# Projection tiles moved to the head of the last stage, gate halves on both sides of the last barrier, and a first gather that reads its indices in place

## The reference

```python
g_logits = hf @ w_rg + b_rg; g_sel = argmax(g_logits)       # one of 4 groups
e_logits = (hf @ w_re + b_re)[group g_sel]                  # 8 experts of it
e_val, e_idx = top_k(e_logits, 2)
gate = softmax(e_val) * softmax(g_logits)[g_sel]
# tokens sorted by expert into blocks; for each block of an expert e:
hid = silu(xe @ w_gate[e]) * (xe @ w_up[e]);  yb = hid @ w_down[e]
x = x + (the two experts' rows of each token, times gate)
gate = sigmoid(rmsnorm(x, g_ple) @ w_ple_gate + b_ple_gate)  # 1024 x 1024
x = x + gate * (p @ w_ple_proj)                              # 256 x 1024
y = rmsnorm(x, g_final)
```

## Time and profile before

| what | value |
|---|---|
| median of three runs | 1224.12 us (1223.11 to 1226.31) |
| the profiled execution | 1224.08 us |
| its span in the trace | 1222.0 us |
| TensorE busy | 1091.6 us (89%) |
| VectorE busy | 528.0 us (43%) |
| ScalarE busy | 489.6 us (40%) |
| GpSimd busy | 240.4 us (20%) |
| moved by DMA | 303.45 MB, mean 248 GB/s |

### The profile page before, as it was taken

How to read it: one execution, slowest core, us unless ns; L and a number is a source line. 1 busy time by engine, 2 the same in 40 slices (tenths; PEclk the granted TensorE clock), 3 DMA queues, 4 the chain that set the end, 5 groups by cost and what they waited for, 6 DMA issues and landing times. The chain is left out here.

```text
span 1222.0 us, 17853 instructions
## 1 busy us (share of the span) xinstructions
PE 1091.6 (89%) x5269; PEld 628.7 (51%) x5270; DVE 528.0 (43%) x687; ACT 489.6 (40%) x667; POOL 240.4 (20%) x280
## 2 busy tenths in 40 slices
PE   3799995689769988899999999999999999949997
PEld 2699995567658764333333333333333333317885
DVE  4458895666832217121321321321221221346886
ACT  4433444433421214343542552552552553523333
POOL 1023564243510011011111111111110110112220
PEclk9899997888969988899999999999999999978999
DMA  6031923201202274699899999999999999984651
GB/s 216 25 106 52 256 68 138 75 35 69 87 18 75 104 283 165 254 395 392 313 395 398 363 397 398 360 397 398 364 397 398 360 397 398 396 346 161 237 190 57
DMA packets 150176, 303.45 MB, mean 248 GB/s; under 512 B 12144, under 2 KB 42896, under 8 KB 150139
## 3 DMA queue, kind: packets, MB, share of 16 engines
q1 hardware_dynamic: 135787, 267.83, 59.8%
q0 software_dynamic: 6512, 22.29, 5.2%
q10 hardware_dynamic: 7840, 12.85, 2.8%
HBM read 262.77 MB, written 40.16 MB: 248 GB/s over the span
## 5 line engine op out<-in xcount | busy, mean ns | idle before, releaser
L1742 PE MATMUL ps_gate_up<-weights,x_turned 128*64 128x512 f32 x1568 | 349.5, 598 | 1.4 <-issue 0.7
L105 ACT COPY weights<-raw_weights 128x2048 f32 (+1 forms) x96 | 180.2, 1899 | 104.3 <-issue 47.4
L105 DVE COPY weights<-raw_weights 128x2048 f32 (+1 forms) x96 | 117.9, 1231 | 228.3 <-PE ps_gate_up L1742 96.4
L1742 PEld LDWEIGHTS ps_gate_up<-weights,x_turned 128*64 128x64 f32 x1568 | 109.5, 137 | 206.9 <-issue 205.8
L1755 PE MATMUL ps_y<-weights,h_turned 128*64 128x512 f32 x784 | 180.7, 603 | 2.4 <-ACT h_turned L1658 2.4
L754 DVE SCALAR_TENSOR_TENSOR taps_bank<-a_ext,par,taps_bank 128x640 f32<-128x640 f32 (+1 forms) x152 | 119.7, 787 | 4.0
L1694 DVE TENSOR_TENSOR hidden<-ps_gate_up,act_gate 128x256 f32<-128x256 f32 x49 | 20.8, 424 | 223.0 <-ACT act_gate L1651 223.0
L395 POOL TENSOR_TENSOR conv_pool_taps<-conv_pool_taps,tap_product 128x640 f32<-128x640 f32 (+1 forms) x64 | 91.7, 1433 | 63.4 <-ACT tap_product L485 57.4
L110 POOL COPY token_ids<-item_tokens 128x1 int32 (+1 forms) x49 | 8.9, 183 | 482.9 <-PE ps_x L1729 457.2
L1755 PEld LDWEIGHTS ps_y<-weights,h_turned 128*64 128x64 f32 x784 | 52.6, 137 | 96.0 <-issue 93.4
L485 ACT ACTIVATE tap_product<-a_ext,par 128x640 f32<-128x640 f32 (+1 forms) x80 | 58.1, 744 | 41.5 <-POOL conv_pool_taps L395 27.5
(11 more groups left out here) (273 smaller groups left out, 1567.2 us busy)
## 6 DMA issues: line engine op xcount, KB each, us to landing
raw_weights<-w_exp_gate SPq DMA_DIRECT2D x128, 512.0 KB, 12.3
raw_weights<-w_exp_up SPq DMA_DIRECT2D x128, 512.0 KB, 12.0
raw_weights<-w_exp_down SPq DMA_DIRECT2D x64, 1024.0 KB, 13.0
y_rows<-y_tile ACTq DMA_DIRECT2D x98, 128.0 KB, 5.4
y_rows<-zero_rows SPq DMA_DIRECT2D x16, 512.0 KB, 6.2
x_rows<-x_tile SPq DMA_DIRECT2D x9, 512.0 KB, 2.6
h_rows<-h_tile SPq DMA_DIRECT2D x9, 512.0 KB, 3.0
proj_rows<-projected SPq DMA_DIRECT2D x9, 512.0 KB, 2.7
```

The lines of the kernel that those rows point to most:

```text
L105: copy(S.work[s][:, :], raw).then_inc(S.w_ready[s], 1)
L1742: last = pe.matmul(ps_gu[side[j], :, :], x_t[:, c, side[of]], w[:, :, share(D_EXP, j)], start=(k == 0), stop=(k == KD - 1))
```

## The change

There is a new constant `LATE = 5`. Tiles 0 to 4 are still projected in `routing`. Tiles 5 to 8 are only transposed there, into a buffer `p_late` that outlives the stage. SyncE then loads the projection's weights a second time, as the first transfer of the expert stage, and `late_project` and `late_leave` multiply and copy out one tile each: tile 5 at the end of the expert stage, tiles 6 to 8 at the head of the last stage. These four are never stored to HBM.

In `routing`, all six pieces of the first expert are now copied by ScalarE, VectorE's chain waits for one GpSimd table instead of all of them, and SyncE's loads of the second expert wait for the last transpose instead of the last projection. In `experts` the last stores of `y` are issued after the copy of `h_turned`, and the engines change places for the gate halves: VectorE makes both halves of pieces 0 and 1 before the barrier, ScalarE the high halves of 2 and 3 before it, and VectorE their low halves after it. The first gather reads its indices from the list without the copy.

```diff
+LATE = 5
 def gather_tokens(pool, S, i):
-    pool.tensor_copy(S.ids[:, :], S.item_tokens[:, bass.ds(i, 1)]).then_inc(S.ids_ready, 1)
-    pool.wait_ge(S.ids_ready, i + 1)
-    pool.sem_inc(S.waits_met, 1)
+    if type(i) is int and i == 0:
+        ids = S.item_tokens[:, 0:1]
+    else:
+        ids = S.ids[:, :]
+        pool.tensor_copy(ids, S.item_tokens[:, bass.ds(i, 1)]).then_inc(S.ids_ready, 1)
+        pool.wait_ge(S.ids_ready, i)
+        pool.sem_inc(S.waits_met, 1)
...
+def gate_lo(dve, S, s):
+    dve.tensor_tensor(S.ple_lo[s][:, :], S.raw[:, 0, s, :], S.ple_hi[s][:, :].bitcast(F32), ALU.subtract).then_inc(S.ple_split, 1)
+
+def late_project(pe, S, t, ps):
+    pe.wait_ge(S.proj_w_loaded, 32)
+    for h in range(2):
+        for k in range(PLE // P):
+            half = slice(h * 512, (h + 1) * 512)
+            last = pe.matmul(ps[:, half], S.p_late[:, t - LATE, k, :], S.late_w[:, k, half], start=(k == 0), stop=(k == PLE // P - 1))
+    last.then_inc(S.late_projected, 1)
+
+def late_leave(act, S, t, ps):
+    act.wait_ge(S.late_projected, t - LATE + 1)
+    act.activation(S.late_rows[t - LATE], ps, ACT.Copy).then_inc(S.late_left, 1)
...
@@ routing, SyncE @@
-                for t in range(T - 1):
+                for t in range(LATE):
                     store(t)
-                sp.wait_ge(projected, 2 * T)
+                sp.wait_ge(projected, 2 * LATE)
+                sp.wait_ge(p_turned, T)
                 for s in (0, 1, 2):
                     load_piece(sp, S, s, 1, 1, slice(1, 2))
-                store(T - 1)
...
@@ routing, TensorE @@
                 for t in range(2, 4):
                     turn_p(t + 1)
                     project(t)
+                turn_p(5)
                 pe.wait_ge(to_place, 1)
                 list_tokens(0)
...
                 pe.matmul(flat_tot[:, 0:ITEMS + 1], owners[:, :], S.ident[:, 0:ITEMS + 1], start=True, stop=True).then_inc(placed, 1)
-                for t in range(5, T):
-                    if t + 1 < T:
-                        turn_p(t + 1)
-                    project(t)
+                for t in range(6, T):
+                    turn_p(t)
...
@@ routing, VectorE @@
-                dve.wait_ge(made, 5)
-                ts(past[:, :], limit[:, 0:SIDES - 1], own_lane[:, :], None, ALU.is_le)
-                red(own_side[:, :], past[:, :], ALU.add)
+                dve.wait_ge(made, 1)
                 dve.wait_ge(S.routed, T)
...
-                for s in (GU[1], GU[3], DOWN[1]):
-                    copy_piece(dve, S, 0, s, None)
...
@@ experts: SyncE first, then the end of ScalarE, VectorE and TensorE @@
+                sp.dma_start(S.late_w[:, :, :], ple_proj).then_inc(S.proj_w_loaded, 16)
...
                 iteration(end, final=True)
-                gate_hi(0)
-                gate_hi(1)
+                gate_hi(2)
+                gate_hi(3)
                 leave_y(end)
+                store_y(end)
+                late_leave(act, S, LATE, ps_late)
...
-                for n, s in enumerate((2, 3)):
+                for n, s in enumerate((0, 1)):
...
-                    gate_lo(s)
-                for s in (0, 1):
-                    dve.wait_ge(S.ple_hi_ready, s + 1)
                     dve.wait_ge(w_ready[DOWN[s]], EXPERTS)
-                    gate_lo(s)
+                    gate_lo(dve, S, s)
...
                 down(end, EXPERTS - 1)
+                late_project(pe, S, LATE, ps_late)
...
@@ embedding_gate, ScalarE @@
+                late_leave(act, S, LATE + 1, ps_g[1][:, :])
+                late_leave(act, S, LATE + 2, ps_h1)
                 to_hi(0)
+                late_leave(act, S, LATE + 3, ps_g[1][:, :])
                 square3(0)
...
@@ embedding_gate, VectorE @@
+                gate_lo(dve, S, 2)
+                gate_lo(dve, S, 3)
+                dve.wait_ge(S.ple_split, 6)
                 combine(0, 0)
...
@@ embedding_gate, TensorE @@
+                late_project(pe, S, LATE + 1, ps_g[1])
+                late_project(pe, S, LATE + 2, ps_h1)
                 turn_h(0, 0)
                 turn_h(0, 1)
+                pe.wait_ge(S.late_left, 2)
+                late_project(pe, S, LATE + 3, ps_g[1])
```

More of the change, by code:

```diff
@@ L95, in load_piece, with copy_piece @@
            .then_inc(S.raw_loaded[s], 16)
-def copy_piece(eng, S, n, s, items):
+def copy_piece(eng, S, n, s, items, on_act=None):
     eng.wait_ge(S.raw_loaded[s], n * LANDED[s] + LANDED[s])
@@ L1472, in _ @@
                 dve.sem_inc(to_exp, 1)
+                ts(past[:, :], limit[:, 0:SIDES - 1], own_lane[:, :], None, ALU.is_le)
+                red(own_side[:, :], past[:, :], ALU.add)
                 dve.wait_ge(ranked, 1)
@@ L1600, in _ @@
                 for j in range(SLOTS):
-                    sp.wait_ge(S.proj_stored[j], 16 * len(range(j, TILES, SLOTS)))
+                    sp.wait_ge(S.proj_stored[j], 16 * len(range(j, LATE, SLOTS)))
                 for t in range(2):
@@ L1656, in iteration @@
                         leave_y(i - 1)
+                        if not final:
+                            store_y(i - 1)
                     act.wait_ge(hid_turned, i + 1)
                     act.activation(h_t[:, :, :], ps_h[:, :, :], ACT.Copy).then_inc(ht_ready, 1)
+                    if final:
+                        store_y(i - 1)
                 def gate_hi(s):
@@ L1704, in _ @@
                 for j in range(SLOTS):
-                    dve.wait_ge(S.proj_stored[j], 16 * len(range(j, TILES, SLOTS)))
-                def gate_lo(s):
-                    dve.tensor_tensor(S.ple_lo[s][:, :], S.raw[:, 0, s, :], S.ple_hi[s][:, :].bitcast(F32), ALU.subtract)\
-                       .then_inc(S.ple_split, 1)
-                for n, s in enumerate((2, 3)):
+                    dve.wait_ge(S.proj_stored[j], 16 * len(range(j, LATE, SLOTS)))
+                for n, s in enumerate((0, 1)):
                     dve.wait_ge(S.raw_loaded[s], LANDED[s] * EXPERTS + 16)
@@ L2132, in build @@
             routing(nc, S)
+        S.late_w = sb("late_ple_proj", [P, PLE // P, D])
+        S.late_rows = [w[:, h * D:(h + 1) * D] for w in S.work[3:5] for h in range(2)]
         S.ple_lo += [sb(f"ple_lo{s}", [P, PIECE], F32R) for s in range(2, 4)]
```

85 lines of the change are left out of this document (54 added, 31 removed).

## The result

Compared on one chip, the changed kernel takes 1215.69 us (median of 5, 1212.61 to 1218.64) and the kernel before 1224.12 (5 runs, 1223.09 to 1226.31). The ratio is 0.9928, with a 95% interval from 0.9905 to 0.9951: faster by 0.7%. The profiled execution took 1214.85 us with a span of 1213.1, against 1224.08 and 1222.0 before. The forecast was 1212.7, with a range from 1209.0 to 1216.0.

A forecast was written before the change was run, and what follows sets the result against it. TensorE was taken to pace the expert loop, with loads running ahead. Routing -15.0, loop 0, loop's end 0 and last stage's head +3.6 sum to -11.4 us: 1224.08 becomes 1212.7, range 1209.0 to 1216.0.

The forecast's parts named there:

- rival 2: Last stage: late gathers make TensorE wait and its clock fall again, +2.0 and up to +1.6 more, 1214.7 to 1216.3; chance 0.15.
- Routing: Routing stage: fewer projections let the second expert's loads and the loop start 15.0 us sooner, bounds 14.2 to 15.7.
- the walk from the earlier trace: Routing: ScalarE's queue added up from 471.6 us to when the last transpose can go, 487.9, or 489.4 with a wait.
- the long case: Routing: tile 2's projection again takes 5.32 us instead of 3.5, so ScalarE waits some 1.5 us: last transpose at 489.4.
- VectorE's earlier chain: Routing: waiting for one table, the chain begins about 3.9 us earlier; about 1.9 us of it arrives at TensorE.
- The loop: Expert loop: TensorE paces it and the 1 MB weight reload is absorbed, 0 us, upper bound 2.7.
- Rival 4: Expert loop: the DMA, not TensorE, sets its end, so an earlier start is worth nothing, 1230.4 us; chance 0.04.
- The end of the loop: Barrier before the last stage: TensorE and VectorE end sooner, but the DMA lands the same bytes; 0, -0.4 to +0.5.
- The held gathers: Head of last stage: VectorE's two subtractions hold GpSimd's first two gathers, rows come 2.1 us later, bounds 0 to 3.7.
- rival 1: Head of last stage: the gathers are not held, leaving only +1.5 us there, 1210.6 us; chance 0.22.
- Tile 8 uncovered and the warm clock: Head of last stage: tile 8 ahead of the first gate product costs +3.5 us; TensorE already warm gives back 2.0.

The follow-up runs named there:

- copies_back: Changed kernel with three of the first expert's six pieces (1, 3 and 5) copied by VectorE again, behind its chain: 1215.6 us against 1225.25 before the change.
- copies_gaps: Changed kernel with pieces 1 and 3 copied by VectorE where its chain waits for TensorE: 1215.71 us against 1225.25 before the change.
- nine: Changed kernel with all nine tiles projected in routing again and none late, the other parts kept: 1226.92 us against 1225.25 before the change.
- rows_mid: Changed kernel with the three broadcasts of gain rows sent in mid loop instead of at its end: 1215.27 us against 1225.35 before the change.
- lo_before: Changed kernel with VectorE's low halves of gate pieces 2 and 3 back ahead of the last barrier: 1213.01 us against 1225.35 before the change.
- after: The changed kernel itself, with all parts of the change: 1215.69 us against 1224.12 for the kernel before.
- tile8_early: Changed kernel with a second late tile at the loop's end and none between transposes and gate products: 1213.27 us against 1225.35 before the change.
- rows_head: Changed kernel with the three broadcasts of gain rows sent at the loop's head, behind the reloaded weights: 1214.84 us against 1225.35 before the change.
- late_w_mid: Changed kernel with the second load of the projection weights (1 MB) sent in mid loop instead of at its head: a single run of 1216.14 us.
- combined: Changed kernel with the edits of lo_before, rows_mid, tile8_early and copies_gaps together: 1208.27 us against 1225.25 before the change, ratio 0.9865.
- abc: The kernel combined without VectorE's two copies in its gaps: 1210.12 us against 1225.18 before the change, ratio 0.9868.

## Why the prediction was right, and where it was off

The direction and the parts that carry the gain were right, and the measured 1215.69 lies in the range of 1209.0 to 1216.0, 0.3 us from its end. It is 3.0 us above the forecast of 1212.7 (the profiled 1214.85 is 2.1 above it) and outside the 1211.5 to 1214 that I had given the forecast alone. The number is the one of rival 2 (1214.7 to 1216.3), whose mechanism did not happen: that the range reached so far up for rival 2 is luck here. Step by step, with what each measured:

- **Routing, -15.0 forecast, -13.7 measured: the term that was mis-sized.** The last transpose starts 33.2 us behind the front end's end, where the walk from the earlier trace rows had given 31.7 to 33.2 (487.9 to 489.4, less 456.19); I took a value near the short end. The 1.5 us that I had put down as the long case is what happened: ScalarE waited 1.71 us for the projection of tile 2, which ran at half clock for most of its 6.12 us, and 0.50 for the next. Of the 1.9 us of VectorE's earlier chain 1.6 arrived (tile 2 starts 15.6 us behind the front end's end, against 17.2). The loop started 4.5 us behind SyncE's load (4.9 forecast). copies_back and copies_gaps show that ScalarE's queue was this stretch's bound, as I had argued: with two or three copies off it, routing is 1.5 to 1.7 us shorter. nine shows that VectorE's earlier chain, the six copies and the missing index copy are together worth nothing without the late tiles.
- **The loop, 0 forecast.** TensorE paces it: its last `ps_y` starts 570.35 us after the loop's start, against 571.95 before, 1.6 us sooner (I had said 1.2). The 1 MB of weights is absorbed: the DMA still moves 385 GB/s over the stretch, and its dry slices come at the same distances from the loop's start as before (some 93, 185, 280, 372 and 465 us). Rival 4 is ruled out.
- **The end of the loop, 0 forecast (-0.4 to +0.5), +1.0 measured: a second mis-sized term, outside its bounds.** That DMA and not TensorE opens this barrier was right, and rows_mid shows it by taking the rows away: -3.6 us. The size was missed by the tail of one engine's rate, of which the trace before shows only 0.5 us (21 GB/s).
- **The held gathers, +2.1 forecast, 1.7 measured** (lo_before against after). The mechanism is the forecast one: the first subtraction ends at about 1083.0 and the first gather at 1083.91; the second ends at 1085.29 and the second gather at 1086.10. The 0.86 us of the earlier trace rows is 0.8 to 0.9 here. The rule of the Trainium skill that I had weighed, "SBUF — State Buffer", section "Who interferes with whom" (`tensor_tensor` with both inputs in SBUF leaves descriptor generation alone, marked there as inferred), would have made this 0. The traces differ: 2.36 and 1.89 us beside such an operation, 0.94 and 0.93 without it, so for such a gather the measurement decides against it, and rival 1 falls. Which part of the gather is held, the reading of its row numbers or the writing of its descriptors, no run separates. nine, with the same two held gathers, lost only 0.8 us over the stage, because its first gate products ran cold for 2.2 us where those of the kernel before did for 4.0.
- **Tile 8 uncovered and the warm clock, +3.5 and -2.0 forecast, so +1.5.** The head took 15.3 instead of 10.9 us up to the first product: 1.7 for the gathers and 2.8 for tile 8, less than the 3.5 forecast, partly since the warm transposes are shorter. The whole stage is only 3.0 longer, so the warm products gave 1.4 back, and 1.3 are left for these two terms. In tile8_early, without the tile, the first product comes 2.3 us sooner but runs cold, and 0.9 us of it stays.
- **Rival 2** did not happen in after, but did in rows_mid (last stage 134.30), at the price that I had given it, 2 to 3.6 us. With waits of 1.05 us ahead of the first transposes and 1.52 ahead of the second the clock stayed up, with 2.16 and 1.06 it was down. Between them the waits do not decide: with 1.60 and 1.52 (rows_head) and 1.73 and 1.52 (late_w_mid) it stayed up, with 1.66 and 1.52 (combined) and 1.72 and 1.52 (abc) it fell ahead of the second transposes. That I gave rival 2 no more than 0.15 was luck as much as reading.

The sum of the measured parts is 0.8 - 13.7 + 1.0 + 3.0 = -8.9 us of span. The forecast was -11.4. The 2.5 us between them are 1.3 in routing, 1.0 at the loop's end and 0.8 in the front end, less the 0.6 by which the last stage beat its +3.6. The front end's +0.8 belongs to no part of the change.

## What to carry over

Work that leaves a stage where it was the bound is worth up to its whole length there, as far as the next bound allows: the four projections took 14.3 us, and after's routing is 13.6 us shorter than nine's. Where it goes decides the rest: look for an idle stretch of the same engine that is closed by someone else, and count what warms up or cools down around it. At a barrier find the party that arrives last before valuing work moved ahead of it or behind it. Here the subtractions had 4 us to spare ahead of the barrier and none behind it, and the barrier's last party was three small broadcasts queued behind a full DMA: moving those to mid loop, the subtractions back and a second late tile ahead of the barrier took the gain from 0.7% to 1.3%.

## What the runs showed of the hardware

- An indirect DMA issued by GpSimd beside a VectorE subtraction with both operands in SBUF took 2.36 and 1.89 us, and 0.94 us without one. It ended 0.8 to 0.9 us behind the subtraction. Of two back-to-back subtractions each held one gather, so a gather gets its turn between them.
- TensorE's granted clock can fall a second time soon after it rose. Behind the loop's first item TensorE waits 2.0 us, transposes for 0.44 and waits 0.7 to 0.8 more. Behind this the clock fell from 1.00 to 0.50, for some 3 us, in copies_back, copies_gaps and combined, and stayed at 1.00 in after and abc, with the same waits. So the waits alone do not decide it. Where it fell the first rise had come sooner: over the second 4 us of the loop the clock was 0.92 in copies_back, 0.89 in copies_gaps and 0.94 in combined, against 0.69 in after and 0.76 in abc.
- The last transfers of a full queue can end at the rate of about one of the 16 DMA engines: 16 to 25 GB/s for 1 us after some 400 GB/s, and the barrier waits for it.
- The same front end took 454.8 to 461.6 us in the eleven profiled executions of the table. A difference of 2 us between two single spans tells nothing here, and between two stages only if the stages around it are alike.
